# Joined two-block kernel: operand order of the passes at each stage's opening, an earlier start, and finer and moved steps beside the products

## The chip, the cores and the metric

One core of a Trainium2 chip. The metric is the device time of one launch in microseconds (us); lower is better. Engines: TensorE (PE), VectorE (DVE), ScalarE (ACT), GpSimd (POOL), and SyncE (SP), whose queue issues the DMAs.

## The reference

Batch 1, sequence 512, width 1024, all f32. Two blocks run one after the other, each of two layers; together they are six sublayers, the kernel's stages. Each takes a norm of x, computes, norms the result and adds it to x.

```python
def first_block(x, ...):                       # layers 0 and 1
        h = rms_norm(x, pre_norm_w[layer])
        y = even_mixer(h, ...)                 # layer 0: retention + stick-breaking attention
        y = odd_mixer(h, ...)                  # layer 1: hgrn2 + causal conv and rg_lru
        x = x + rms_norm(y, post_norm_w[layer])
def second_block(x, ...):                      # sandwich(h, pre, post, fn) = h + rmsnorm(fn(rmsnorm(h)))
    h = sandwich(h, ..., even_mixer_2)         # differential attention + conformer convolution
    h = sandwich(h, ..., swiglu)               # (silu(h @ w_gate) * (h @ w_up)) @ w_down, 1024 -> 2816 -> 1024
    h = sandwich(h, ..., odd_mixer_2)          # S5 state-space layer (256 channels) + latent attention, 6 heads
    h = sandwich(h, ..., swiglu)
```

The parts that the change touches: every projection `h @ w_in`; in `s5_ssm` the discretisation (`mag`, `cos`, `sin` of `li * dt`) and the linear recurrence over time of 1024 complex states; in `mla_attention` the softmax of each head, `softmax(q k^T)`, over key blocks of 64.

## The kernel before

The activations stay on chip, transposed: features on 128 partitions, 8 tiles `k` of 128 × 512. The weights come once, as a stream of 128 × 128 tiles in slots of 8 (512 KB): SP loads a slot into one of three buffers `raw`; ScalarE rounds it to fp32r, `wh` (`round_slot`, L624 to L630); GpSimd computes the remainder `wl = raw − wh` in four pieces (`split_slot`, L2627 to L2631). Activations are treated alike: `hh` is x times the norm's weight, rounded (ScalarE, L645), `hl` its remainder (VectorE, L693); inside a stage `mh`, `ml`. One product of a 128 × 128 weight tile with 512 tokens is three matmuls (passes) into one PSUM bank, in `product`, L569 to L578:

```python
            e.matmul(ps[b][:], a, xh, start=first, stop=False)
            e.matmul(ps[b][:], a, xl, start=False, stop=False)
            e.matmul(ps[b][:], l, xh, start=False, stop=final).then_inc(pe.sem, pe.up(*step))
```

The order of all work is a list of steps per stage (`STEPS`, from `steps_even`, `steps_odd`, `steps_diff`, `steps_ffn`, `steps_ssm`), written by hand. Every engine walks the same list and issues its share of each step into its own in-order queue; engines meet at semaphores alone. A step `("w", g, k)` is one product of group g (128 output features), `("e", g)` the eviction of g's bank, `claim` makes TensorE wait until the bank's last reader is done, and `BANKS` says which of eight banks a kind of group may use. `merge` (L96) interleaves lists evenly by their length, so that a list with more steps is spread at other places. The stages are `even`, `odd`, `diff`, `ffn0`, `ssm`, `ffn1`.

**Opening** (L133). Each stage begins with x's update by the stage before (`nx`, VectorE L679 and L682), then for each k: `hi` (ScalarE: `hh`, and the square of x, L645 and L648), `lo` (VectorE: `hl`), the products of three groups (two in ssm), and `sq`, a matmul of ones by the square (L605), which sums for the norm; `rs` turns the sum into a factor that the evictions apply. Block k means these steps of one k. TensorE waits for `lo` of k ahead of block k. The sums and evictions go to banks 0 to 3 and 7.

**Start of the kernel.** ScalarE (`scalar_program`, L2613) rounds the first three slots, then waits for `mats` (a table of 128 × 128 constants) and copies five of them to fp32r (`EXACT`, L2619), then enters `act_even`, which loads its function table (L981) and comes to `hi` 0. SP (`sync_program`, L2656) issues x in eight transfers, a slot after x1, x3 and x7, and `mats` after x3.

**ffn0.** Gate and up products (`fg`, `fu`) for a tile f, their evictions (`e1` to `e3`) beside the next tile's products, down products, and the closing (`o`, then `on`, the ones matmul of the post-norm). The eight steps `ds` compute the S5 layer's tables (VectorE, ScalarE, GpSimd) for the stage after; they are merged into the closing of ffn0.

**ssm.** Per pair of attention heads: projections `un`, `ur`, `kn`, `vw`; for two lanes at a time score products `r1` (L2123 to L2128), row maximum `r2` (VectorE L2335) and exponentials (ScalarE L2499), reciprocal `r3` (L2340, L2342), transposing products `r4` (L2137), values `v1`, `v2`. Beside it the scan over eight sets of 128 states: `s1` (TensorE L2158, L2159; VectorE L2356 to L2359, products with cosine and sine), `s2` (two sums L2365, L2367; two scans L2369, L2371), `s3` (four products and two sums, L2377 to L2386), `s4` (TensorE L2170, L2172), and after each four sets `z1` to `z4`, which end in the input of `zg`, the gate's product. Heads and scan are merged.

## Time and profile before

| | |
|---|---|
| median of 3 runs | 2041.15 us (2040.47 to 2041.37) |
| the profiled execution's own time | 2041.19 us |
| its span, first to last instruction | 2039.4 us |
| mean granted TensorE clock | 0.934 |
| busy: PE, PEld | 1795.7 us (88%) of 7412 matmuls, 1350.4 us (66%) |
| busy: DVE, ACT, POOL | 960.8 us (47%), 738.5 us (36%), 926.9 us (45%) |
| DMA | 139.89 MB, mean 69 GB/s |

The table is from one profiled execution. PE is the matmul itself and PEld its weight load, which overlaps with it. Busy shares are means over stages of different kinds; what bounds a place is read from the waits in it. The stages take roughly: even 0 to 340 us, odd to 660, diff to 950, ffn0 to 1335, ssm to 1645, ffn1 to the end. The granted clock is a share of full speed; its two levels are 1.2 and 2.4 GHz. In waits, "PE ps L576 <- DVE hl L693" is TensorE idle ahead of a matmul of line 576, released by the instruction of line 693 on VectorE.

### The profile page before, as it was taken

Reading aid. Unit: us, or ns where it says so; the run is one execution under the profiler, and the core shown is the slowest. Engines: PE = TensorE matmul, PEld = TensorE weight load, DVE = VectorE, ACT = ScalarE, POOL = GpSimd, SP = SyncE. Lnnn points to the kernel's source line nnn. Section 1 sums busy time; section 2 is a strip of 40 time slices with the busy share of each in tenths; the row PEclk is TensorE's granted clock in tenths of the full one; section 3 lists DMA queues with packets and bytes.
Section 4 is the critical chain, followed back from the end, with each engine's and each line's share of the span. In section 5 each row is a group of like instructions: output and inputs, shape, how many; then the busy total and the mean of one; then the engine's idle time right before and its main releaser. Section 6 shows DMA issues by size and latency. Waiting matters only on the chain.

```text
span 2039.4 us, 19949 instructions
## 1 busy us (share of the span) xinstructions
PE 1795.7 (88%) x7412; PEld 1350.4 (66%) x7412; DVE 960.8 (47%) x1483; ACT 738.5 (36%) x1207; POOL 926.9 (45%) x1100
## 2 busy tenths in 40 slices
PE   5999978988778888688999999978777889999996
PEld 3776556666665676456788888755444568888885
DVE  1043435675543699636321313655655554123244
ACT  4264554354344322454332222342222443322232
POOL 3433124465653444024565656467123336556563
PEclk9999999988988899898999999997778899999998
DMA  4311012122111122012232332211000112233231
GB/s 169 93 63 63 31 42 82 62 63 72 42 32 52 62 73 73 11 42 73 85 102 93 98 99 94 77 60 49 11 11 21 42 63 93 94 100 96 93 97 69
DMA packets 39553, 139.89 MB, mean 69 GB/s; under 512 B 4512, under 2 KB 4640, under 8 KB 39328
## 3 DMA queue, kind: packets, MB, share of 16 engines
q1 hardware_dynamic: 39456, 138.61, 21.3%
q8 instruction: 59, 0.97, 0.2%
q14 instruction: 38, 0.31, 0.1%
HBM read 136.50 MB, written 2.10 MB: 68 GB/s over the span
## 4 chain that ended last, share of the span: by engine, by line
PE 72%; DVE 17%; ACT 7%; issue 2%; POOL 1%; DMA 0%; SPq 0%; DVEq 0%; ACTq 0%; POOLq 0%
PE ps L576 18%; PE ps L577 18%; PE ps L578 18%; DVE ps L1734 3%; PE ps L605 2%; PE ps L589 1%; PE ps L2146 1%; PE ps L591 1%; PE ps L590 1%; PE ps L841 1%; PE ps L2123 1%; POOL wl L2631 1%; PE ps L1150 1%; PE ps L2137 1%; DVE arena L679 1%
## 5 line engine op out<-in xcount | busy, mean ns | idle before, releaser
L2631 POOL TENSOR_TENSOR wl<-raw,wh 128x256 fp32r<-128x256 f32 x988 | 802.8, 843 | 975.8 <-ACT wh L630 975.4
L576 PE MATMUL ps<-hh,wh 128*128 128x512 f32 x1204 | 518.3, 431 | 72.8 <-DVE hl L693 46.0
L577 PE MATMUL ps<-hl,wh 128*128 128x512 f32 x1204 | 479.1, 398 | 0.0
L578 PE MATMUL ps<-hh,wl 128*128 128x512 f32 x1204 | 478.7, 398 | 0.0
L630 ACT ACTIVATE wh<-raw 128x1024 fp32r<-128x1024 f32 x247 | 261.0, 1057 | 559.6 <-PE ps L578 511.2
L576 PEld LDWEIGHTS ps<-hh,wh 128*128 128x128 f32 x1204 | 232.9, 193 | 150.7 <-DVE hl L693 52.1
L576 PE MATMUL ps<-mh,wh 128*128 128x512 f32 x632 | 267.8, 424 | 48.5 <-DVE ml L937 7.8
L577 PEld LDWEIGHTS ps<-hl,wh 128*128 128x128 f32 x1204 | 232.7, 193 | 62.0 <-issue 17.7
L578 PEld LDWEIGHTS ps<-hh,wl 128*128 128x128 f32 x1204 | 232.0, 193 | 50.6
L577 PE MATMUL ps<-ml,wh 128*128 128x512 f32 x632 | 254.0, 402 | 0.0
L578 PE MATMUL ps<-mh,wl 128*128 128x512 f32 x632 | 253.8, 402 | 0.0
L576 PEld LDWEIGHTS ps<-mh,wh 128*128 128x128 f32 x632 | 123.2, 195 | 98.2 <-issue 12.1
L578 PEld LDWEIGHTS ps<-mh,wl 128*128 128x128 f32 x632 | 123.2, 195 | 27.1
L577 PEld LDWEIGHTS ps<-ml,wh 128*128 128x128 f32 x632 | 124.2, 196 | 23.8 <-issue 1.9
L1944 DVE TENSOR_TENSOR ml<-arena,mh 128x512 fp32r<-128x512 f32 x44 | 35.0, 795 | 119.4 <-ACT mh L1975 119.4
L1933 DVE TENSOR_TENSOR arena<-ps,nrm 128x512 f32<-128x512 f32 x44 | 30.4, 691 | 127.7 <-PE ps L578 127.7
L1734 DVE SCALAR_TENSOR_TENSOR ps<-arena,vec,ps 128x512 f32<-128x512 f32 x116 | 87.4, 753 | 2.9
L1931 DVE TENSOR_TENSOR arena<-ps,nrm 128x512 f32<-128x512 f32 x44 | 29.9, 680 | 100.0 <-PE ps L578 100.0
L693 DVE SCALAR_TENSOR_TENSOR hl<-x,vec,hh 128x512 fp32r<-128x512 f32 x48 | 40.2, 838 | 54.1 <-ACT hh L645 54.1
L589 PE MATMUL ps<-wh,hh 128*128 128x512 f32 x128 | 51.9, 405 | 9.3 <-DVE arena L1205 9.2
L661 ACT ACTIVATE nrm<-arena 128x512 f32<-128x512 f32 x48 | 30.1, 627 | 77.2 <-DVE arena L703 77.1
L605 PE MATMUL ps<-nrm,mats 128*128 128x512 f32 x96 | 53.4, 640 | 0.0
(464 smaller groups left out, 2223.6 us busy)
## 6 DMA issues: line engine op xcount, KB each, us to landing
raw<-in_w SPq DMA_DIRECT2D x247, 512.0 KB, 3.5
x<-in_x SPq DMA_DIRECT2D x8, 256.0 KB, 6.9
out<-x SPq DMA_DIRECT2D x8, 256.0 KB, 2.0
arena<-in_rope SPq DMA_DIRECT2D x3, 512.0 KB, 4.9
arena<-in_dec SPq DMA_DIRECT2D x1, 1024.0 KB, 11.3
mats<-in_mats SPq DMA_DIRECT2D x1, 576.0 KB, 7.9
arena<-in_lw SPq DMA_DIRECT2D x1, 512.0 KB, 3.8
arena<-in_levels SPq DMA_DIRECT2D x1, 448.0 KB, 4.5
```

The costliest lines, as they stand in the source:

```text
L576: e.matmul(ps[b][:], a, xh, start=first, stop=False)
L577: e.matmul(ps[b][:], a, xl, start=False, stop=False)
L578: e.matmul(ps[b][:], l, xh, start=False, stop=final).then_inc(pe.sem, pe.up(*step))
L589: e.matmul(ps[i][:], hh[:, k, cut(i)], a, start=(k == 0), stop=False)
L605: e.matmul(ps[7][:], M("ones"), sqr[k % 2], start=(k == 0), stop=(k == KT - 1)).then_inc(pe.sem, pe.up("sq", k))
L630: e.activation(wh[:, n % NHL, :], raw[:, n % NRAW, :], ACT.Copy).then_inc(rounded.sem, rounded.up(n))
L661: e.activation(sqr[d % 2], y[:, d, :], ACT.Square).then_inc(act.sem, act.up("oe", d))
L693: e.scalar_tensor_tensor(out=hl[:, k, :], in0=x[:, k, :], scalar=V(PRE[stage], k), in1=hh[:, k, :].bitcast(F32), op0=MUL, op1=SUB).then_in ...
L1734: e.scalar_tensor_tensor(out=yb[:, j, :] if q == 30 else conv_in[j], in0=du[:, j, q:q + T], scalar=V("dww", 4 * q + j), in1=conv_in[j], op ...
L1933: e.tensor_tensor(f_up[f % 2], ps[bank(stage, ("fu", f))][:], rb_pre, MUL).then_inc(dve.sem, dve.up("e", ("fu", f)))
L1944: e.tensor_tensor(ml[:, i, :], f_up[f % 2], mh[:, i, :].bitcast(F32), SUB).then_inc(dve.sem, dve.up("mixed", f))
L2631: e.tensor_tensor(wl[:, n % NHL, cut(i, 2)], raw[:, n % NRAW, cut(i, 2)], wh[:, n % NHL, cut(i, 2)].bitcast(F32), SUB).then_inc(split.sem, ...
```

## The change

1. **Openings.** In each block k of the opening of all six stages, the passes of the two or three groups are ordered by operand: first `wh`·`hh` of each group, then `wh`·`hl` of each, then `wl`·`hh` of each. The first kind waits for `hi` of k and, at a slot's start, for the rounding alone; the second for `lo` of k; the third, at a slot's start, for `wl`. Consecutive passes go to different banks.
2. **Start.** ScalarE loads the function table ahead of any wait; the three slots are rounded between the `hi` steps, the copies of `EXACT` stand ahead of `hi` 4. TensorE waits for these copies at the last ones matmul of the first stage instead of the first. SP issues a slot after x0, x1 and x3, and `mats` after x1's slot.
3. **ffn0.** The `ds` steps go into the gate and up groups of tiles 0 to 3, 5 and 7 to 9. The table preloaded at the end of step 4 is another one.
4. **ssm.** `s1` is cut in two steps, `s2` and `s3` in three each, and the list of the scan is ordered by hand around them. `merge` then places the pieces at other points between the heads' steps; the stage's list has 417 steps where it had 377.
5. **Banks.** In odd, the groups `gl`, `gg`, `hq` and `hf` may use banks 0 to 3 instead of 0 and 1.

The lists of even, odd, diff and ffn1 are as before.

```diff
@@ open_products, new; it is called at each stage's first "w" step of block k
+        def open_products(e, stage, k):
+            s, gs = S[stage], OPENS[stage]
+            e.wait_ge(s.act.sem, s.act["hi", k])
+            for g in gs:
+                step = ("w", g, k)
+                if k == 0:
+                    claim(e, bank(stage, g))
+                if (stage, step) in STARTS:
+                    e.wait_ge(rounded.sem, rounded[STARTS[stage, step]])
+                e.matmul(ps[bank(stage, g)][:], tile(stage, step)[0], hh[:, k, :], start=(k == 0), stop=False)
+            e.wait_ge(s.dve.sem, s.dve["lo", k])
+            for g in gs:
+                e.matmul(ps[bank(stage, g)][:], tile(stage, ("w", g, k))[0], hl[:, k, :], start=False, stop=False)
+            for g in gs:
+                step = ("w", g, k)
+                if (stage, step) in STARTS:
+                    e.wait_ge(split.sem, split["wl", STARTS[stage, step]])
+                e.matmul(ps[bank(stage, g)][:], tile(stage, step)[1], hh[:, k, :], start=False, stop=(k == KT - 1)).then_inc(
+                    s.pe.sem, s.pe.up(*step))
+                if k == KT - 1:
+                    busy[bank(stage, g)] = (s.dve, ("e", g))
@@ pe_norms, "sq"
                     if stage == "even":
                         e.wait_ge(s_mats, 16)
-                        e.wait_ge(consts.sem, consts[EXACT[-1]])
+                if stage == "even" and k == KT - 1:
+                    e.wait_ge(consts.sem, consts[EXACT[-1]])
@@ act_even (the preload and the loops leave scalar_program, whose first line is now the preload)
-            e.preload_act_table_set(EXP_LN)
...
+                if kind == "hi" and 1 <= step[1] <= NHL:
+                    round_slot(e, step[1] - 1)
+                if step == ("hi", NHL + 1):
+                    e.wait_ge(s_mats, 16)
+                    for name in EXACT:
+                        e.activation(R(name), M(name), ACT.Copy).then_inc(consts.sem, consts.up(name))
@@ sync_program
-                if k in (1, 3, 7):
-                    load_slot(e, k // 3)
-                if k == 3:
+                if k in (0, 1, 3):
+                    load_slot(e, (k + 1) // 2)
+                if k == 1:
                     e.dma_start(mats[:], io["mats"]).then_inc(s_mats, 16)
@@ STEPS
-"ffn0": steps_ffn(*[("ds", n) for n in range(8)]),
+"ffn0": steps_ffn(first=[("ds", 0)], f1=[("ds", 1)], f2=[("ds", 2)], f3=[("ds", 3)], f5=[("ds", 4)], f7=[("ds", 5)],
+                  f8=[("ds", 6)], f9=[("ds", 7)]),
@@ steps_ssm
-        scan += [("s1", i), ("s2", i), ("s1", i + 1), ("s3", i), ("s2", i + 1), ("s3", i + 1)]
+        scan += [("s1", i), ("s1b", i), ("s2", i), ("s2b", i), ("s1", i + 1), ("s1b", i + 1), ("s2c", i), ("s3", i), ("s3b", i)]
+        scan += [("s3c", i), ("s2", i + 1), ("s2b", i + 1), ("s2c", i + 1), ("s3", i + 1), ("s3b", i + 1), ("s3c", i + 1)]
@@ BANKS, "odd"
-"gl": (0, 1), "gg": (0, 1), "hq": (0, 1), "hf": (0, 1)
+"gl": (0, 1, 2, 3), "gg": (0, 1, 2, 3), "hq": (0, 1, 2, 3), "hf": (0, 1, 2, 3)
```

`s1b` holds the third and fourth product of `s1`, `s2b` and `s2c` the two scans, `s3b` the third and fourth product of `s3`, `s3c` its two sums.

**The queues.** TensorE at the kernel's start, block 0, before:

```order
L576 MATMUL ps0<-hh,wh 128x512 [waits weights_split,dve_even]
L577 MATMUL ps0<-hl,wh 128x512
L578 MATMUL ps0<-hh,wl 128x512
L576 MATMUL ps1<-hh,wh 128x512
L577 MATMUL ps1<-hl,wh 128x512
L578 MATMUL ps1<-hh,wl 128x512
L576 MATMUL ps2<-hh,wh 128x512
L577 MATMUL ps2<-hl,wh 128x512
L578 MATMUL ps2<-hh,wl 128x512
L605 MATMUL ps7<-nrm,mats 128x512 [waits act_even,constants_set,mats_landed]
```

and now:

```order
L599 MATMUL ps0<-hh,wh 128x512 [waits weights_rounded,act_even]
L599 MATMUL ps1<-hh,wh 128x512
L599 MATMUL ps2<-hh,wh 128x512
L602 MATMUL ps0<-hl,wh 128x512 [waits dve_even]
L602 MATMUL ps1<-hl,wh 128x512
L602 MATMUL ps2<-hl,wh 128x512
L607 MATMUL ps0<-hh,wl 128x512 [waits weights_split]
L607 MATMUL ps1<-hh,wl 128x512
L607 MATMUL ps2<-hh,wl 128x512
L638 MATMUL ps7<-nrm,mats 128x512 [waits act_even,mats_landed]
```

The same ten matmuls; those with `hl` and with `wl` now stand behind three that need neither, and the wait for all constants is off the first ones matmul.

ScalarE at the kernel's start, before:

```order
L630 ACT_TABLE_LOAD [waits weights_landed0]
L630 ACTIVATE wh<-raw 128x1024 [waits constants_set]
L630 ACTIVATE wh<-raw 128x1024 [waits weights_landed1]
L630 ACTIVATE wh<-raw 128x1024 [waits weights_landed2]
L2619 ACTIVATE mats_exact<-mats 128x128 [waits mats_landed]
L2619 ACTIVATE mats_exact<-mats 128x128 x4
L981 ACT_TABLE_LOAD [waits vec_landed]
L645 ACTIVATE hh<-x,vec 128x512 [waits x0_landed]
L648 ACTIVATE nrm<-x 128x512
L645 ACTIVATE hh<-x,vec 128x512 [waits x1_landed]
```

and now (L678 and L681 are `hi`, L663 the rounding):

```order
L2680 ACT_TABLE_LOAD
L678 ACTIVATE hh<-x,vec 128x512 [waits x0_landed,vec_landed,constants_set]
L681 ACTIVATE nrm<-x 128x512
L663 ACTIVATE wh<-raw 128x1024 [waits weights_landed0]
L678 ACTIVATE hh<-x,vec 128x512 [waits x1_landed]
L681 ACTIVATE nrm<-x 128x512
L663 ACTIVATE wh<-raw 128x1024 [waits weights_landed1]
L678 ACTIVATE hh<-x,vec 128x512 [waits x2_landed]
L681 ACTIVATE nrm<-x 128x512 [waits pe_even]
L663 ACTIVATE wh<-raw 128x1024 [waits weights_landed2]
L678 ACTIVATE hh<-x,vec 128x512 [waits x3_landed]
```

`hh` 0 stood behind two table loads, three roundings and five copies, and is now the second instruction; the roundings stand between the `hh`, and the copies of `mats` follow behind a fourth rounding, ahead of `hh` 4.

TensorE in ssm, where the second `s1` (L2158, L2159; now L2206, L2207) stands, before:

```order
L576 MATMUL ps0<-mh,wh 128x512 [waits act_ssm]
L577 MATMUL ps0<-ml,wh 128x512
L578 MATMUL ps0<-mh,wl 128x512
L2158 MATMUL ps6<-arena 128x512 [waits dve_ssm]
L2159 MATMUL ps7<-arena 128x512
L576 MATMUL ps0<-mh,wh 128x512
L577 MATMUL ps0<-ml,wh 128x512
L578 MATMUL ps0<-mh,wl 128x512
L2123 MATMUL ps2<-arena 128x384 [waits act_ssm,dve_ssm]
L2123 MATMUL ps3<-arena 128x384
```

and now:

```order
L587 MATMUL ps0<-mh,wl 128x512
L585 MATMUL ps1<-mh,wh 128x512 [waits dve_ssm]
L586 MATMUL ps1<-ml,wh 128x512
L587 MATMUL ps1<-mh,wl 128x512
L2206 MATMUL ps6<-arena 128x512 [waits dve_ssm]
L2207 MATMUL ps7<-arena 128x512
L2131 MATMUL ps0<-wh,mh 128x128 [waits weights_split,act_ssm]
L2132 MATMUL ps0<-wl,mh 128x128
L2133 MATMUL ps0<-wh,ml 128x128
```

It stood inside the products `un` of the second pair of heads, behind the first scores; it now stands behind the last `kn` of the first pair, ahead of `vw` (L2131 to L2133) and all scores.

VectorE in ssm, ahead of the row maxima (L2335; now L2383) of the third pair of score blocks; L2377 to L2386 is `s3` of the second set, now L2436 to L2452. Before:

```order
L2340 RECIPROCAL small<-small 128x1 [waits act_ssm]
L2342 TENSOR_SCALAR nrm<-mats,small 128x128 [waits dve_ssm]
L2377 TENSOR_TENSOR hh_scratch_49<-hh_scratch_49,mh_scratch_51 128x512 [waits dve_ssm]
L2379 TENSOR_TENSOR hl_scratch_50<-hl_scratch_50,mh_scratch_51 128x512 [waits dve_ssm]
L2381 TENSOR_TENSOR hl_scratch_50<-hl_scratch_50,ml_scratch_52 128x512 [waits dve_ssm]
L2382 TENSOR_TENSOR hh_scratch_49<-hh_scratch_49,ml_scratch_52 128x512
L2384 TENSOR_TENSOR hh_scratch_49<-hh_scratch_49,hl_scratch_50 128x512 [waits dve_ssm]
L2386 TENSOR_TENSOR hl_scratch_50<-hl_scratch_50,hh_scratch_49 128x512 [waits dve_ssm]
L2340 RECIPROCAL small<-small 128x1 [waits act_ssm]
L2342 TENSOR_SCALAR nrm<-mats,small 128x128 [waits dve_ssm]
L2335 TENSOR_REDUCE small<-ps2 128x1 [waits pe_ssm]
L2335 TENSOR_REDUCE small<-ps3 128x1 [waits pe_ssm]
```

and now:

```order
L2390 TENSOR_SCALAR nrm<-mats,small 128x128 [waits dve_ssm]
L2430 SCALAR_TENSOR_TENSOR hl_scratch_50<-small,hl_scratch_50 128x512 [waits dve_ssm]
L2388 RECIPROCAL small<-small 128x1 [waits act_ssm]
L2390 TENSOR_SCALAR nrm<-mats,small 128x128 [waits dve_ssm]
L2436 TENSOR_TENSOR hh_scratch_49<-hh_scratch_49,mh_scratch_51 128x512 [waits dve_ssm]
L2438 TENSOR_TENSOR hl_scratch_50<-hl_scratch_50,mh_scratch_51 128x512 [waits dve_ssm]
L2444 TENSOR_TENSOR hl_scratch_50<-hl_scratch_50,ml_scratch_52 128x512 [waits dve_ssm]
L2445 TENSOR_TENSOR hh_scratch_49<-hh_scratch_49,ml_scratch_52 128x512
L2383 TENSOR_REDUCE small<-ps2 128x1 [waits pe_ssm]
L2450 TENSOR_TENSOR hh_scratch_49<-hh_scratch_49,hl_scratch_50 128x512 [waits dve_ssm]
L2452 TENSOR_TENSOR hl_scratch_50<-hl_scratch_50,hh_scratch_49 128x512 [waits dve_ssm]
L2383 TENSOR_REDUCE small<-ps3 128x1 [waits pe_ssm]
```

The first row maximum moves ahead of the two sums of `s3`, the second stays behind all six instructions.

## Rows read from the trace of the kernel before

**Rows 1.** The page's part 4, whole span: share by engine.
```profile
PE 72%; DVE 17%; ACT 7%; issue 2%; POOL 1%; DMA 0%; SPq 0%; DVEq 0%; ACTq 0%; POOLq 0%
```

**Rows 2.** Waits of TensorE, whole span: us in total, times, longest.
```profile
PE ps L576 <- DVE hl L693: 46.0, 6, 21.0
PE ps L2123 <- ACT nrm L2499: 27.6, 6, 6.4
```

**Rows 3.** Timeline, kernel's start: start us, us, engine line, output <- inputs [idle before <- releaser].
```profile
7.72 1.28 ACT L630 ACT_TABLE_LOAD   x1 [7.72 <-DMA raw<-in_w]
...
10.15 5.49 POOL L2631 TENSOR_TENSOR wl<-raw,wh 128x256 fp32r<-128x256 f32 x8 [9.71 <-ACT wh L630]
...
19.39 0.72 ACT L645 ACTIVATE hh<-x,vec 128x512 fp32r<-128x512 f32 x1
...
21.03 0.79 PE L576 MATMUL ps<-hh,wh 128*128 128x512 f32 x1 [21.03 <-DVE hl L693]
...
25.95 0.96 PE L576 MATMUL ps<-hh,wh 128*128 128x512 f32 x1
```

**Rows 4.** The tile mats, 0 to 60: from issue to landing, us.
```profile
DMA to landing us min/median/max: 7.9/7.9/7.9
```

**Rows 5.** DMA view, 0 to 60, in 40 slices of 1.5 us.
```profile
GB/s 0 221 184 300 325 405 418 398 410 411 431 415 404 344 289 85 0 0 0 0 0 0 0 0 60 289 0 0 11 38 292 19 0 0 0 82 265 3 0 33
```

**Rows 6.** Timeline, opening of the stage odd.
```profile
339.70 0.72 ACT L645 ACTIVATE hh<-x,vec 128x512 fp32r<-128x512 f32 x1 [1.54 <-DVE x L682]
...
341.77 0.79 PE L576 MATMUL ps<-hh,wh 128*128 128x512 f32 x1 [5.00 <-DVE hl L693]
...
355.75 0.80 PE L576 MATMUL ps<-hh,wh 128*128 128x512 f32 x1
...
358.70 0.80 PE L576 MATMUL ps<-hh,wh 128*128 128x512 f32 x1
```

**Rows 7.** Windows: stretch, sum, PE, PEld, DVE, ACT, POOL busy, PEclk, DMA share, GB/s.
```profile
337.00:347.00 10.00, 5.23 (x12) 3.81 (x12) 8.67 (x11) 5.17 (x8) 3.65 (x4) 0.67 0.29 98
```

**Rows 8.** The same view, body of ffn0.
```profile
1100.00:1150.00 50.00, 50.00 (x222) 41.41 (x221) 16.95 (x22) 13.78 (x18) 30.84 (x36) 1.00 0.30 95
```

**Rows 9.** Waits of TensorE, 1290 to 1345, closing of ffn0.
```profile
PE ps L576 <- DVE arena L703: 2.8, 3, 1.6
PE ps L576 <- POOL wl L2631: 1.7, 2, 1.0
PE ps L616 <- DVE nrm L711: 1.3, 1, 1.3
```

**Rows 10.** Windows view and timeline, ssm, the merged heads and scan.
```profile
1395.00:1612.00 217.00, 171.26 (x587) 103.99 (x586) 132.60 (x216) 54.83 (x122) 64.48 (x60) 0.77 0.06 18
...
1419.30 0.69 DVE L2356 TENSOR_TENSOR hh_scratch<-ps,mh_scratch 128x512 f32<-128x512 f32 x1 [6.37 <-PE ps L2159]
...
1440.64 0.75 DVE L2335 TENSOR_REDUCE small<-ps 128x1 f32<-128x256 f32 x2
...
1443.04 0.55 PE L2123 MATMUL ps<-arena 128*128 128x128 f32 x1 [5.02 <-ACT nrm L2499]
...
1487.49 0.98 PE L2123 MATMUL ps<-arena 128*128 128x384 f32 x1 [5.35 <-ACT nrm L2499]
...
1544.24 0.56 PE L2123 MATMUL ps<-arena 128*128 128x384 f32 x1 [3.48 <-ACT nrm L2499]
...
1570.42 0.55 PE L2123 MATMUL ps<-arena 128*128 128x128 f32 x1 [6.37 <-ACT nrm L2499]
```

**Rows 11.** Timeline of VectorE, ssm, first and last of the last z chain.
```profile
1598.48 0.75 DVE L2392 SCALAR_TENSOR_TENSOR arena<-arena,vec,ps 128x512 f32<-128x512 f32 x1 [3.06 <-PE ps L2172]
...
1611.90 1.15 DVE L2414 TENSOR_TENSOR hl<-arena,hh 128x512 fp32r<-128x512 f32 x1 [0.70 <-ACT hh L2532]
```

**Rows 12.** Timeline of TensorE, stage odd, two waits for an eviction.
```profile
477.40 0.80 PE L589 MATMUL ps<-wh,hh 128*128 128x512 f32 x1 [9.02 <-DVE arena L1205]
...
532.68 0.80 PE L576 MATMUL ps<-hh,wh 128*128 128x512 f32 x1 [5.61 <-DVE arena L1205]
```

82 lines of the change are left out of this document (55 added, 27 removed), and 2 rows, old and new, of the table BANKS.

## Prediction

> **What bounds the kernel now.** I read the chain of waits first. TensorE holds 72% of the chain that ended last, VectorE 17%, ScalarE 7% [rows 1]: this is a matmul-bound kernel with holes, and only two things save time, fewer holes in TensorE's work or a clock that is granted in full for longer. Next, TensorE's waits, to see which holes there are. The largest is `product` waiting for `hl`, the remainder of the activations, 46.0 us in six times of which one is 21.0 [rows 2]. So the start of the kernel costs 21.0 and each of the five later stage openings 5.0. Second is the wait for the softmax exponentials in the ssm stage, 27.6 us in six. Third I read one window per place that the change touches.
>
> **Start of the kernel.** ScalarE sits until the first weights are there (7.72), loads a table, rounds three slots, waits for `mats`, copies it, loads a second table, and comes to the first `hh` at 19.39; TensorE starts at 21.03 and leaves block 0 at 25.95 [rows 3]. Only the first slot is needed for that block.
>
> Now: the table load comes before any wait, `hh` 0 needs only x0, then slot 0 is rounded. x0, half as large, stands right ahead of slot 0 in SP's queue, so `hh` 0 and its square are done before the weights come. One x less (256 KB) stands ahead of slot 0 than before, and the transfers run at 300 to 430 GB/s without a break from 4.5 to 21 us [rows 5], so its landing moves from 7.7 to about 7.2. Rounding 1.06 gives 8.3: the three passes of rounded weights with `hh` start there, the three with `hl` follow (6 × 0.43 slow-clock passes = 2.6, to 10.9), and the weights' remainder is there at 8.3 + 4 × 0.69 (5.49/8 in [rows 3]) = 11.05. Three passes more end at 12.35. The ones matmul needs `mats`: it is issued behind x1 and slot 1, two x earlier than before, near 3.1, and 7.9 from issue to landing [rows 4] give 11.0, no wait. It takes 1.05 (21.03 to 25.95 is 4.92, less nine passes of 0.43), so block 1 starts at 13.4 instead of 25.95: 12.55 earlier.
>
> A part is given back at block 4. `hh` 4 now stands behind the rounding of slot 3 and the five copies of `mats`. Slot 3's raw data is about 6 MB down the queue, at 410 GB/s some 16 us, and with its start and the pauses of the queue 19 to 20; + 1.06 (a rounding) + 1.1 (five small copies, taken as one rounding) + 0.72 = 21.9 to 22.9 for `hh` 4, and TensorE gets there at 13.4 + 3 × 2.95 = 22.25. I take 0.55 of stall. **−12.0**, bounds −10.5 (slot 0 lands at 8.8, the stall 1.1) and −13.
>
> **Openings.** [Rows 6] show the second stage's; the four others look the same. ScalarE has `hh` 0 at 340.42; TensorE starts at 341.77, released by `hl` 0, after 5.00 of idling. Its passes are 0.43 apart at first (341.77 to 346.69 for block 0, as long as at the kernel's start), which is 1.2 GHz, and 0.23 later, 2.4 GHz; the granted clock is 0.67 over 337 to 347 [rows 7]. Full-speed blocks are 355.75 to 358.70, 2.95 apart, and never wait: from block 1 on `hh` and `hl` are ahead. So all that the new pass order releases is the first block's head. Three passes need only `hh`: they start at 340.48 instead of 341.77, run 3 × 0.43 = 1.29, and `hl` is there as they end. Four openings × 1.29 and ssm's, with two groups, 0.86: **−6.0**. The clock falls as before, since TensorE still idles 3.7, and recovers as much earlier as work starts earlier. Bounds: if it recovered at the old moment, the early passes would save only half, −3. If it did not fall at all, each opening would save another 2.3 (9 × 0.20 plus half of the ones matmul's 1.05), together −17.5.
>
> Later blocks write banks 0, 1, 2 in turn instead of three passes each. What does a change of bank cost? The ffn body changes bank at each product's end, and 222 matmuls fill its 50.00 us [rows 8]: 0.225 each, where 512 columns at 2.4 GHz are 0.213. If all of the 0.012 excess were bank changes, one in three matmuls, a change would be 0.036, and the 272 added ones 9.8 us. But a block of the openings, with a change at one pass in three, is no slower per pass than the body: 2.95 [rows 6] less a ones matmul of two half-rate passes (0.9) is 0.228 for each of nine. I take 0, with 9.8 as bound. The Trainium skill, "TensorE: Matmul & The Clock Gate", section "A second HAM failure mode: psum-queue depth-cycling", speaks against this order: a kernel that cycles through PSUM banks each iteration had TensorE idling briefly so often that its clock went up and down. The body's row, cycling at every third pass with the clock at 1.00, does not show it; at every pass no run here shows it. By that rule it is the slower rival below.
>
> **ffn0.** The eight `ds` steps stood in the closing, where TensorE waited 2.8 for `arena`, 1.7 for `wl` and 1.3 for `nrm` [rows 9], waits that ffn1's closing, the same without `ds`, does not have. They move under gate and up groups, where TensorE is busy 50.00 of 50.00 while VectorE is at 34% and ScalarE at 28% [rows 8]. **−5.8**, bounds −4 and −6. If that cover failed, the `e` steps would free banks later and nothing would be gained. The other table preloaded replaces one load by one: 0.
>
> **ssm.** The window 1395 to 1612 holds the merged heads and scan: TensorE idles 46 of 217 us at clock 0.77 [rows 10]. The waits come from VectorE's in-order queue: the row maxima (reduces) at 1440.64 stand behind two scans and six products of the scan, the exponentials wait for them and TensorE for those, 5.02 at 1443.04. Before that VectorE had idled 6.37 waiting for TensorE's two s1 matmuls (1419.30): they now stand ahead of the first `vw` and the first scores, so that work is done while VectorE had none, and in pieces of one or two instructions the first reduce of a pair stands two products earlier. Walking the gaps 1443.04, 1487.49, 1544.24, 1570.42 [rows 10] (20.2 together) in the new order: −3.4, −4, −2.5, −3.5, together −13.4. Against it: s1 ahead of the first `vw` delays the first scores by their two matmuls at slow clock, +1.5, and the last z chain starts later: today it runs 1598.48 to 1611.90 [rows 11] beside the output products, and its end releases `zg`; about 2 of it would come out from cover. **−10**, bounds −25 (the clock recovers too over part of the window) and +5.
>
> **odd banks.** Gates and hq/hf get four banks for two. TensorE waited 9.02 and 5.61 for `arena` [rows 12], evictions that freed a bank; but what sets the pace there is VectorE's own chain, so most of that returns at the next need. I take **−3**, bounds 0 and −12.
>
> **Sum.** 12.0 + 6.0 + 5.8 + 10 + 3 = 36.8 off the profiled execution's 2041.19 (0.04 above the median of the runs): **2004.4**, say 2004.
>
> **Rivals.**
> 1. The ssm reorder and the banks bring next to nothing, because VectorE's busy sum there (132.6 of 217 [rows 10]) is unchanged and each released wait is met at the next in-order step (the second reduce of the pair at 1440.64 still stands behind all six products). Start, openings and ffn0 remain: 23.8, 2017; with part of it, 2013 to 2022. For it: these are the terms got by walking, not by a row. 0.22.
> 2. ssm backfires: z's chain exposed in full, 13.4 [rows 11], or a scan standing before each reduce. 2041.2 − 23.8 + 5 to 13: 2022 to 2032. 0.08.
> 3. The pass order releases nothing, since another wait (bank, rounded weights) ends as late: 6 less and part of the start, 2010 to 2017. 0.04.
> 4. The clock: with idling cut from 5.0 to 3.7 the openings may keep it, −11.5, and ssm at 0.77 has room, its 171 busy us shrinking by up to 10 at a fuller clock. 1980 to 1995. 0.18.
> 5. Slower: changing banks at every pass makes TensorE pause, and the clock goes with it. The openings' 408 passes would run at 0.43 instead of 0.225: 83.7 us dearer, 2088. It decides from 36.8/408 = 0.09 us per pass on. Against it are the body's rows. 0.03.
> Mine, 1995 to 2013, gets 0.45. A measurement of this kernel can tell about 0.2% (4 us) from no change, so 2037 to 2045 is "same": 0.01, only by a partial rival 5. Faster 0.95, slower 0.04. The range, 1983 to 2025, takes in rivals 1 and 3, most of 4 and a third of 2.
>
> **What would show it.** TensorE's wait for `hl` should all but vanish and be replaced by one for `hh`, 3.7 per opening; the first matmul at 8.3 and block 1 at 13.4; blocks still 2.95 apart (more than 3.3 is rival 5); ffn0's three closing waits gone; TensorE's busy time unchanged within 5 us and ssm's window at about 205 instead of 217. I am wrong if ssm's waits for the exponentials stay at 27 (rival 1), if the wait for `zg` after the last z chain exceeds 8 (rival 2), or if the first matmul comes later than 10.

## The result, and the profile after

The changed kernel takes 2005.74 us (median of 4, 2000.34 to 2006.59) against 2041.26 (median of 4): ratio 0.9819, interval 0.9801 to 0.9838, 35.5 us faster. The forecast was 2004, in 1983 to 2025. The profiled execution took 2006.59 us, its span is 34.6 us shorter than before's.

The page of the changed kernel, its head and the chain that ended last:

```profile
span 2004.8 us, 19949 instructions
...
PE 1793.1 (89%) x7412; PEld 1346.4 (67%) x7412; DVE 969.6 (48%) x1483; ACT 738.6 (37%) x1206; POOL 931.4 (46%) x1100
...
PE 72%; DVE 16%; ACT 6%; POOL 2%; issue 2%; DMA 1%; SPq 0%; DVEq 0%; ACTq 0%; POOLq 0%
```

TensorE's share of the chain is the same as in [rows 1], of a shorter span. Its waits over the whole span (us in total, times, longest):

```profile
PE ps L599 <- ACT hh L678: 20.1, 6, 3.7
...
PE ps L2171 <- ACT nrm L2565: 12.9, 6, 4.2
...
PE ps L2171 <- ACT arena L2565: 10.6, 3, 7.1
...
PE ps L621 <- DVE arena L1247: 8.8, 1, 8.8
...
PE ps L585 <- POOL wl L2693: 8.7, 3, 5.3
...
PE ps L599 <- ACT wh L663: 7.8, 1, 7.8
```

The wait for `hl` of [rows 2] is gone; 20.1 for `hh` and 7.8 for the first rounded slot stand in its place. The exponentials of ssm held TensorE for 27.6 and now hold it for 12.9 in one form and 10.6 in the other, which was 1.5 before. Of the 8.7 for the weights' remainder, all in odd, before has nothing; its own 1.7 [rows 9] were in ffn0 and are gone.

Where the 34.6 us came from. I took two milestones of each stage in both traces: the last sum of its opening (the small matmul of the step `rs`, L610, now L643) and the ones matmul of its post-norm (L616, now L649), and how much earlier each comes:

| milestone | before | now | earlier by | gained since the line above | forecast |
|---|---|---|---|---|---|
| even, opening's end | 48.60 | 37.86 | 10.74 | 10.74 | 12.0 |
| even, post-norm | 333.98 | 326.64 | 7.34 | −3.40 | 0 |
| odd, opening's end | 369.54 | 360.02 | 9.52 | 2.18 | 1.29 |
| odd, post-norm | 658.06 | 648.13 | 9.93 | 0.41 | 3 |
| diff, opening's end | 693.59 | 681.22 | 12.37 | 2.44 | 1.29 |
| diff, post-norm | 944.91 | 931.41 | 13.50 | 1.13 | 0 |
| ffn0, opening's end | 980.50 | 964.52 | 15.98 | 2.48 | 1.29 |
| ffn0, post-norm | 1331.28 | 1307.75 | 23.53 | 7.55 | 5.8 |
| ssm, opening's end | 1360.71 | 1336.80 | 23.91 | 0.38 | 0.86 |
| ssm, post-norm | 1641.25 | 1607.88 | 33.37 | 9.46 | 10 |
| ffn1, opening's end | 1676.83 | 1642.32 | 34.51 | 1.14 | 1.29 |
| ffn1, post-norm | 2021.46 | 1986.91 | 34.55 | 0.04 | 0 |

The start, in the timeline of the changed kernel (start us, us, engine line, [idle before <- releaser]):

```profile
6.57 1.06 ACT L663 ACTIVATE wh<-raw 128x1024 fp32r<-128x1024 f32 x1 [0.54 <-DMA raw<-in_w]
...
7.77 1.62 PE L599 MATMUL ps<-hh,wh 128*128 128x512 f32 x3 [7.77 <-ACT wh L663]
...
11.01 1.65 PE L607 MATMUL ps<-hh,wl 128*128 128x512 f32 x3 [0.34 <-POOL wl L2693]
...
13.01 1.26 PE L599 MATMUL ps<-hh,wh 128*128 128x512 f32 x3
...
21.22 1.06 ACT L663 ACTIVATE wh<-raw 128x1024 fp32r<-128x1024 f32 x1 [4.07 <-DMA raw<-in_w]
...
22.18 1.09 ACT L1024 ACTIVATE mats_exact<-mats 128x128 fp32r<-128x128 f32 x5
...
23.94 0.98 PE L599 MATMUL ps<-hh,wh 128*128 128x512 f32 x3 [1.59 <-ACT hh L678]
```

TensorE starts at 7.77 where [rows 3] have 21.03, waits 0.34 for the weights' remainder, and is at block 1 at 13.01 instead of 25.95. Of these 12.9 us, 1.59 are given back at block 4, behind the fourth rounding (21.22) and the constants (22.18).

The opening of odd, in the timeline:

```profile
333.14 1.35 PE L599 MATMUL ps<-hh,wh 128*128 128x512 f32 x3 [3.70 <-ACT hh L678]
...
337.51 1.27 PE L599 MATMUL ps<-hh,wh 128*128 128x512 f32 x3
```
and in the windows view (stretch, its length, busy us of PE, PEld, DVE, ACT and POOL, PEclk, DMA share, GB/s):

```profile
328.37:338.37 10.00, 6.30 (x15) 3.68 (x16) 7.38 (x10) 5.63 (x9) 2.35 (x3) 0.83 0.32 112
```

TensorE idles 3.70 instead of 5.00 [rows 6], and block 0 lasts 4.37 us (333.14 to 337.51) instead of 4.92: the clock is back sooner. The ten microseconds that begin 4.77 before TensorE's start have a granted clock of 0.83; [rows 7] are the same ten around before's opening, 0.67. From one stage's post-norm to the next opening's end, the windows view of before has granted clocks of 0.90 (odd, diff, ffn0, ffn1) and 0.88 (ssm); now they are 0.95 in odd, diff and ffn0, and 0.90 in ffn1 and 0.88 in ssm as before.

ffn0's closing and the start of ssm's opening, TensorE's waits from 1265 to 1320; the three of [rows 9] are gone, and one of 0.6 behind the post-norm's first ones matmul is new:

```profile
PE ps L599 <- ACT hh L678: 3.7, 1, 3.7
PE ps L651 <- ACT nrm L694: 0.6, 1, 0.6
```

In ssm, the stretch from the opening's end to the post-norm, first before, then now (windows view):

```profile
1360.71:1641.25 280.54, 227.27 (x815) 147.10 (x816) 159.83 (x249) 82.06 (x157) 108.24 (x108) 0.82 0.09 29
```

```profile
1336.80:1607.88 271.08, 223.59 (x814) 145.00 (x815) 164.51 (x249) 82.31 (x157) 112.12 (x108) 0.83 0.10 30
```

280.54 us with 53.3 of idle TensorE became 271.08 with 47.5. One of the waits that grew, in the timeline of the changed kernel:

```profile
1401.14 1.55 DVE L2450 TENSOR_TENSOR hh_scratch<-hh_scratch,hl_scratch 128x512 f32<-128x512 f32 x1
...
1402.61 1.74 DVE L2452 TENSOR_TENSOR hl_scratch<-hl_scratch,hh_scratch 128x512 f32<-128x512 f32 x1
...
1405.27 0.55 DVE L2383 TENSOR_REDUCE small<-ps 128x1 f32<-128x384 f32 x1
...
1405.73 1.08 DVE L2416 TENSOR_TENSOR hh_scratch<-hh_scratch 128x512 f32<-128x512 f32 x1
...
1406.74 1.75 DVE L2418 TENSOR_TENSOR hl_scratch<-hl_scratch 128x512 f32<-128x512 f32 x1
...
1408.40 0.55 DVE L2383 TENSOR_REDUCE small<-ps 128x1 f32<-128x384 f32 x1
...
1409.04 0.58 ACT L2565 ACTIVATE arena<-ps,small 128x384 f32<-128x384 f32 x1 [2.53 <-DVE small L2383]
...
1409.82 2.04 PE L2171 MATMUL ps<-arena 128*128 128x256 f32 x4 [7.11 <-ACT arena L2565]
```

L2383 is the row maximum, L2416 and L2418 are sums of the scan, L2450 and L2452 the last of the set before. The second maximum of the pair (1408.40) stands behind the two sums (1405.73 and 1406.74), the first (1405.27) behind the two before; the exponentials follow and TensorE has idled 7.11, where the same matmul waited 1.11 before (at 1431.74). It is the kind of wait that [rows 10] show at 1443.04, at another pair.

### The profile page after: what moved, and what is told of

Its sections match the earlier page's. It is cut to its first block, busy times and chain, and to the rows that moved or that the text cites. A ratio compares the mean times of both kernels' runs of the same rounds, so it can differ in the third digit from the quotient of the medians.

```text
span 2004.8 us, 19949 instructions
## 1 busy us (share of the span) xinstructions
PE 1793.1 (89%) x7412; PEld 1346.4 (67%) x7412; DVE 969.6 (48%) x1483; ACT 738.6 (37%) x1206; POOL 931.4 (46%) x1100
## 4 chain that ended last, share of the span: by engine, by line
PE 72%; DVE 16%; ACT 6%; POOL 2%; issue 2%; DMA 1%; SPq 0%; DVEq 0%; ACTq 0%; POOLq 0%
PE ps L585 17%; PE ps L587 17%; PE ps L586 17%; DVE ps L1778 4%; PE ps L638 2%; PE ps L602 2%; PE ps L599 2%; PE ps L607 2%; POOL wl L2693 1%; PE ps L621 1%; PE ps L622 1%; PE ps L623 1%; PE ps L876 1%; PE ps L2171 1%; PE ps L2194 1%
## 5 line engine op out<-in xcount | busy, mean ns | idle before, releaser
L663 ACT ACTIVATE wh<-raw 128x1024 fp32r<-128x1024 f32 x247 | 260.9, 1057 | 573.4 <-PE ps L587 512.6
L585 PE MATMUL ps<-hh,wh 128*128 128x512 f32 x1068 | 441.3, 413 | 21.7 <-POOL wl L2693 8.7
L586 PE MATMUL ps<-hl,wh 128*128 128x512 f32 x1068 | 421.5, 395 | 0.0
L587 PE MATMUL ps<-hh,wl 128*128 128x512 f32 x1068 | 421.3, 394 | 0.0
L586 PEld LDWEIGHTS ps<-hl,wh 128*128 128x128 f32 x1068 | 204.5, 191 | 46.4 <-issue 6.8
L587 PEld LDWEIGHTS ps<-hh,wl 128*128 128x128 f32 x1068 | 203.7, 191 | 44.0
L587 PEld LDWEIGHTS ps<-mh,wl 128*128 128x128 f32 x632 | 123.5, 195 | 27.3
L599 PE MATMUL ps<-hh,wh 128*128 128x512 f32 x136 | 61.3, 559 | 27.9 <-ACT hh L678 20.1
L599 PEld LDWEIGHTS ps<-hh,wh 128*128 128x128 f32 x136 | 27.4, 207 | 55.5 <-issue 27.3
```

What stands on the lines that cost most here:

```text
L599: e.matmul(ps[bank(stage, g)][:], tile(stage, step)[0], hh[:, k, :], start=(k == 0), stop=False)
L663: e.activation(wh[:, n % NHL, :], raw[:, n % NRAW, :], ACT.Copy).then_inc(rounded.sem, rounded.up(n))
```

## The experiments

Twelve kernels. Medians of one kernel differ by up to 3.5 us between sets of runs (before: 2041.8, 2044.7, 2041.3, 2043.2 in the four sets, and 2037 to 2047 in single runs), so where a part is worth a few us I read the stretches of its trace.

**The start alone.** The edits of point 2 of the change, on the kernel before, with the old `product` in the openings.

```diff
+            e.preload_act_table_set(EXP_LN)
             e.wait_ge(consts.sem, consts["set", 2])
-            for n in range(NHL):
-                round_slot(e, n)
...
-                if k in (1, 3, 7):
-                    load_slot(e, k // 3)
+                if k in (0, 1, 3):
+                    load_slot(e, (k + 1) // 2)
```

> The start's part alone (table load first, roundings between the hi steps, slots and constants issued earlier), with the old pass order. Theory: TensorE must still wait for the weights' remainder of slot 0, so it starts near 11 instead of 7.8, block 1 near 15.9 instead of 25.95, and nothing stalls at block 4, because hh 4 (ready near 24) comes before TensorE does: 10.0 us faster than before. Rival (the start gains only with the new pass order, since the remainder is what is late): under 5 us. Second rival: the stall at block 4 is there as well and limits the gain to the 10.7 of the whole change, so both are within 1 us of one another.

2030.24 us against 2041.8, ratio 0.9938 (0.9915 to 0.9961). Its timeline:

```profile
11.27 0.77 PE L582 MATMUL ps<-hh,wh 128*128 128x512 f32 x1 [11.27 <-POOL wl L2639]
...
15.36 0.80 PE L582 MATMUL ps<-hh,wh 128*128 128x512 f32 x1
...
25.26 0.50 PE L582 MATMUL ps<-hh,wh 128*128 128x512 f32 x1 [0.56 <-DVE hl L700]
```

TensorE waits for the weights' remainder till 11.27 and is at block 1 at 15.36; block 4 (25.26) waits 0.56 for `hl`. At the opening's end it is 9.91 us ahead of before, the changed kernel 10.74. The theory has the size (10.0) but said that nothing stalls at block 4; the second rival, a stall there as well and the two kernels within 1 us, holds. The new pass order starts TensorE 3.5 us sooner and brings block 1 forward by 2.35, and at block 4 the changed kernel stalls 1.59 where this one stalls 0.56. The other 7 us by which this profiled execution was ahead came in ssm, which it does not touch; see below.

**The pass order alone.** `open_products` in all six openings, on the kernel before.

```diff
-                    if g == ("lx", 0):
-                        e.wait_ge(dve.sem, dve["lo", k])
+                    if g in OPENS["odd"]:
+                        if g == OPENS["odd"][0]:
+                            open_products(e, "odd", k)
+                        continue
```

> The new pass order in all six openings alone. Forecast's term: 6.0 us faster, 1.29 in each of four openings and 0.86 in ssm, plus about 0.9 at the kernel's start, 6.9 in all. Theory after the trace of the whole change, where the openings of odd, diff and ffn0 gave 2.2 to 2.5 each: block 0 also ends its slow stretch sooner, so 8.5 to 9.5. Rival (a change of bank costs 0.036 us a pass): 9.8 less, no gain or slower.

2034.17 us against 2041.8, ratio 0.9955 (0.994 to 0.9971): 7.6 us faster by the medians, 9.2 by the ratio. By milestones the openings gave 0.91, 2.45, 2.07, 2.43, 0.92 and 2.43, together 11.2; 1.9 were lost in the body of odd. So an opening is worth more than the 1.29 us of its three early passes, and the granted clock tells where: in odd, diff, ffn0 and ffn1, from post-norm to opening's end, it is 0.95 here for before's 0.90. ffn1's opening shows both cases in the eight kernels with this order: 1.98 to 2.43 us gained in the four whose clock there is 0.95, and 1.14 to 1.41, about the early passes alone, in the four with 0.90.

**Banks in turn, old waits.** The same order of passes, but nothing may start earlier. The lines are against the kernel of the pass order alone; the later waits for `lo` and for `wl` go.

```diff
-            e.wait_ge(s.act.sem, s.act["hi", k])
+            e.wait_ge(s.dve.sem, s.dve["lo", k])
...
-                    e.wait_ge(rounded.sem, rounded[STARTS[stage, step]])
+                    e.wait_ge(split.sem, split["wl", STARTS[stage, step]])
```

> The same order of passes, but each block waits for what it waited for before (hl and the weights' remainder ahead of its first pass), so that only the turning of banks is left of this part. Theory: a change of bank is free, within 1 us of before, blocks of the openings 2.95 us apart at full clock as before. Rival (TensorE pauses at each change of bank): up to 9.8 us slower than before, a block 3.2 us; with the clock going down as well, over 80 us slower.

2042.66 us (10 runs) against 2041.8 (13 runs), ratio 1.0002 (0.9992 to 1.0012). Its timeline in the opening of odd:

```profile
354.71 1.26 PE L596 MATMUL ps<-hh,wh 128*128 128x512 f32 x3
...
357.65 1.26 PE L596 MATMUL ps<-hh,wh 128*128 128x512 f32 x3
```

A block at full clock takes 2.94 us (354.71 to 357.65), the 2.95 of [rows 6]. A change of bank at every pass costs nothing that can be measured, and the granted clock of the openings is before's (0.90, ssm 0.88); the slower rival falls. The case of the Trainium skill that the prediction weighed ("TensorE: Matmul & The Clock Gate", "A second HAM failure mode: psum-queue depth-cycling") is another one: there TensorE idled briefly between groups of matmuls, while here the banks change inside an unbroken run of passes.

The surprise is elsewhere: at the even stage's post-norm this kernel is 4.55 us behind before, though it was 0.72 ahead at the opening's end and nothing differs in between. The same stretch in three kernels (before, this one, the changed kernel), which run the same list of instructions there:

```profile
48.60:333.98 285.38, 265.74 (x1117) 187.20 (x1117) 98.12 (x195) 130.89 (x240) 98.31 (x132) 0.97 0.19 59
```

```profile
47.88:338.53 290.65, 270.99 (x1117) 189.99 (x1117) 98.23 (x195) 130.95 (x240) 98.26 (x132) 0.95 0.18 58
```

```profile
37.86:326.64 288.78, 269.36 (x1116) 189.06 (x1117) 98.12 (x195) 130.98 (x240) 98.23 (x132) 0.96 0.19 59
```

TensorE idles 19.6, 19.7 and 19.4 us in them, and the same waits last equally long in each; but it is busy 265.7, 271.0 and 269.4 us for the same matmuls, with a granted clock of 0.97, 0.95 and 0.96. After each wait of some microseconds a slow stretch follows or does not, and how long it is changes from execution to execution. This is the 3.40 that the change seems to lose in even. The kernel of the next experiment shows it more plainly: up to ffn0 it is before itself, and its even stretch is 290.59 us with 19.7 idle, 5.2 longer. In its trace 27.3 us of that stretch stand at 1.2 GHz, in before's 17.1; half of the difference is 5.1. Over all fourteen traces the stretch takes 283.4 to 290.6 us (mean 287.6), so before's is a short one.

**ds alone.** Point 3 of the change.

```diff
-"ffn0": steps_ffn(*[("ds", n) for n in range(8)]),
+"ffn0": steps_ffn(first=[("ds", 0)], f1=[("ds", 1)], f2=[("ds", 2)], f3=[("ds", 3)], f5=[("ds", 4)], f7=[("ds", 5)],
+                  f8=[("ds", 6)], f9=[("ds", 7)]),
```

> The ds steps alone moved from ffn0's closing into its gate and up groups. Forecast's term: 5.8 us faster. The trace of the whole change shows 7.55 for the stretch from ffn0's opening to its post-norm; if all of that is this part, 7.5. Rival (the evictions beside the gate and up products get late and the gain is half lost): 3 us or less.

2032.53 us against 2041.8, ratio 0.995 (0.9935 to 0.9965). The stretch from ffn0's opening to its post-norm is 7.55 us shorter, to the hundredth what the changed kernel shows; 0.63 is given back right behind, where the second ones matmul of the post-norm now waits. The body takes the steps without a gap:

```profile
1100.00:1150.00 50.00, 50.00 (x223) 41.40 (x222) 21.57 (x34) 14.71 (x18) 30.76 (x36) 1.00 0.32 96
```

VectorE's share is 43% where [rows 8] have 34%, TensorE is busy 50.00 of 50.00. The 7.55 are more than the 5.87 us that TensorE idles there before. The rest is in the matmuls next to each wait, as the trace of before shows at the first one:

```profile
1304.47 0.39 PE L578 MATMUL ps<-mh,wl 128*128 128x512 f32 x1
1305.91 0.50 PE L576 MATMUL ps<-mh,wh 128*128 128x512 f32 x1 [1.04 <-DVE arena L703]
1306.25 0.40 PE L577 MATMUL ps<-ml,wh 128*128 128x512 f32 x1
```

Starts are 0.23 apart in an unbroken run. Here they are 1.44 and 0.34 apart, 1.78 for two steps that take 0.46 without a wait: 1.32 us for an idle time of 1.04. The five waits inside the products cost 0.27 us each beyond their idle time, 1.4 together; the sixth is ahead of the post-norm.

**The scan alone.** Point 4 of the change.

```diff
-        scan += [("s1", i), ("s2", i), ("s1", i + 1), ("s3", i), ("s2", i + 1), ("s3", i + 1)]
+        scan += [("s1", i), ("s1b", i), ("s2", i), ("s2b", i), ("s1", i + 1), ("s1b", i + 1), ("s2c", i), ("s3", i), ("s3b", i)]
+        scan += [("s3c", i), ("s2", i + 1), ("s2b", i + 1), ("s2c", i + 1), ("s3", i + 1), ("s3b", i + 1), ("s3c", i + 1)]
```

> The scan's steps cut and reordered, alone. Forecast's term: 10 us faster. Theory after reading five traces whose ssm list is the old one (TensorE idles 52.8 to 54.3 us between the openings' last sum and the post-norm of that stage, in 273.5 to 280.5 us, a spread of 7 that no edit explains) and the whole change's (47.5 us idle in 271.0): the reorder removes 6 us of idling and the stretch takes 269 to 273 us, so about 6 us faster by medians, with 7.11 still idle at a wait for the exponentials of the second pair. Rival (all 9.5 us seen in the trace are the reorder's): the stretch at 267 or less. Rival (the clock gave them all): idling stays above 52.

2034.22 us against 2044.73, ratio 0.995 (0.9932 to 0.9968). The stretch of ssm:

```profile
1363.35:1634.41 271.06, 223.97 (x815) 145.25 (x815) 164.35 (x249) 82.30 (x157) 111.86 (x108) 0.83 0.10 31
```

271.06 us with 47.1 idle, the changed kernel's 271.08 and 47.5. The six kernels that keep the old list take 273.6 to 280.5 us there (mean 277.5) with 52.8 to 54.3 idle. The three kernels with the new list as it stands take 271.06 to 271.32. So by the traces the reorder is worth 6.4 us of that stretch, as the theory had it, and the remaining 3 of the 9.46 are before's own execution, one of the two longest. The medians say more, 10.5 us, with an interval of 6.5 to 13.9 by the ratio: the traces' figure lies at its lower end.

**The banks alone.** Point 5.

```diff
-"gl": (0, 1), "gg": (0, 1), "hq": (0, 1), "hf": (0, 1)
+"gl": (0, 1, 2, 3), "gg": (0, 1, 2, 3), "hq": (0, 1, 2, 3), "hf": (0, 1, 2, 3)
```

> Four banks for gl, gg, hq and hf in the odd stage, alone. Forecast's term: 3 us faster, bounds 0 and 12. Theory after the trace of the whole change: TensorE runs ahead at once, and there waits 8.7 us in three times for the weights' remainder (GpSimd), which it had not waited for before; the waits for evictions only change places, so within 0.5 us of before at the odd stage's post-norm.

2041.67 us (10 runs) against 2044.73 (13 runs), ratio 0.999 (0.998 to 0.9999). TensorE's waits from 365 to 600:

```profile
PE ps L1156 <- DVE arena L1350: 10.0, 11, 3.0
...
PE ps L595 <- DVE arena L1211: 8.8, 1, 8.8
...
PE ps L582 <- POOL wl L2637: 8.4, 3, 5.3
```

The two of [rows 12] are among six waits for L1205's evictions before, 22.5 us; one of 8.8 is left. In their stead TensorE waits 8.4 us for GpSimd's remainder, before 0, and 10.0 for another eviction (L1350), before 3.7. The odd stage, from its opening's end to its post-norm, takes 288.79 us, before 288.52. The part alone gives nothing in its own stretch; the 3 us between the medians, with an interval that just excludes 0, have no place in it.

**Late rounding and constants**, an attempt to take back the stall at block 4 of the changed kernel.

```diff
-                round_ahead(e, "even", step)
+                if STARTS.get(("even", step)) != 1:
+                    round_ahead(e, "even", step)
...
-                if step == ("hi", NHL + 1):
+                if step == ("hi", 6):
+                    round_slot(e, NHL)
+                if step == ("hi", 7):
```

> The changed kernel with the fourth rounding put behind hi 6's place and the five copies of constants ahead of hi 7, so that hi 4 and hi 5 no longer stand behind them. Theory: the 1.59 us of TensorE at block 4 go, and with them all that the start gave back: block 8's end 1.6 us earlier than in the changed kernel, nothing later gets late, since slot 3 is used first behind the opening. Rival (another thing holds block 4, the square or the x transfer): less than 0.5 us.

2003.89 us, ratio 0.9801 (0.9782 to 0.982); the opening's end 12.03 us ahead of before, the changed kernel's 10.74:

```profile
14.00 1.30 PE L599 MATMUL ps<-hh,wh 128*128 128x512 f32 x3
...
22.85 1.26 PE L599 MATMUL ps<-hh,wh 128*128 128x512 f32 x3
```

Block 4 starts 8.85 us after block 1, without a wait, where the changed kernel took 10.93 (13.01 to 23.94). The first slot landed later in this execution (block 1 at 14.00), so that of the 2.1 us 1.29 are seen at the opening's end. Executions differ here as well: the opening's end is 10.45 to 11.81 us ahead of before in the three kernels with the early rounding, and 11.85 to 13.11 in the four with the late one.

**The scan behind the row maxima**, on the changed kernel: every piece of the scan and of z that stands between a score product `r1` and the second row maximum `r2` of its pair moves behind that maximum.

```diff
+def behind_rows(steps):
+    out = list(steps)
+    for n in range(0, 24, 2):
+        a, b = out.index(("r1", n)), out.index(("r2", n + 1))
+        part = out[a:b + 1]
+        late = [v for v in part if v[0] in ("s1", "s1b", "s2", "s2b", "s2c", "s3", "s3b", "s3c", "s4", "z1", "z2", "z3", "z4")]
+        out[a:b + 1] = [v for v in part if v not in late] + late
+    return out
...
-    out += merge(mul, scan)
+    out += behind_rows(merge(mul, scan))
```

> The changed kernel with the scan's pieces that stand between a score product and the second row maximum of its pair put behind that maximum, in all twelve pairs. Theory: what TensorE waits for in ssm are the maxima behind scan work on VectorE, so its two kinds of waits ahead of the scores (12.9 and 10.6 us in the changed kernel) fall to under 15 together, and the stage is 5 to 8 us shorter. Rival (VectorE's sum of work sets the pace, 149 of 232 us, and the wait moves to the scan's own chain): the scores' waits fall, but others grow by as much, 0 to 2 us.

1988.8 us, ratio 0.9728 (0.9705 to 0.9751), 17 us off the changed kernel. Its waits from 1331 to 1587:

```profile
PE ps L2195 <- ACT arena L2583: 7.5, 9, 3.2
...
PE ps L2181 <- ACT nrm L2575: 7.1, 3, 5.5
...
PE ps L2195 <- DVE nrm L2400: 4.0, 2, 2.9
...
PE ps L2181 <- ACT arena L2575: 2.1, 3, 1.2
```
and its stretch of ssm:

```profile
1331.04:1586.95 255.91, 215.79 (x814) 140.46 (x815) 164.26 (x249) 81.44 (x157) 109.77 (x108) 0.86 0.10 33
```

The two waits ahead of the scores are 7.1 and 2.1 where they were 12.9 and 10.6, others grew (7.5 for the eviction ahead of the transposing products, 4.0 for the reciprocals), idling is 40.1 for 47.5, and the stretch is 15.2 us shorter, twice what the idling says: TensorE's busy time fell by 7.8 us as well, at a clock of 0.86 for 0.83. This is more than the 5 to 8 us expected.

**Both**, the late rounding and the scan behind the row maxima.

> The two improvements together: the late fourth rounding and constants, and the scan's pieces behind the row maxima. Theory: they act 1300 us apart and add up, 1.6 + 15.2 us off the changed kernel by their own stretches, 1988 to 1990 where the changed kernel has 2005.7. Rival (the clock's dips move and take part back): anything up to 5 us off that, with the stretch of the scan still at 254 to 258 us and TensorE's idle time there at 40.

1991.84 us, ratio 0.9754 (0.9733 to 0.9775). The stretch of ssm is 255.77 us with 38.9 idle, the opening's end 12.24 us ahead; both parts are there. The even stage took 288.11 us where the kernel above had 283.39, and diff's 3.5 more, both untouched. The median lies 2 us above the theory's 1988 to 1990, inside what the rival on the clock allowed.

**The scan uncut, behind the row maxima.** The same rule, on the changed kernel with point 4 undone (the steps s1, s2, s3 whole and in their old order).

> The changed kernel with the scan's steps uncut, in the order before, but with every piece of the scan between a score product and the second maximum of its pair put behind that maximum. Theory: what counts is what a maximum stands behind, not how fine the scan's steps are: the stage's stretch is within 4 us of the 255.9 of the cut list with the same rule, idling 40 to 44. Rival (the cut matters by itself, since whole steps hold up the reciprocals and the values between two maxima): over 264.

1980.66 us, ratio 0.9709 (0.9688 to 0.973). Its stretch of ssm:

```profile
1333.21:1579.29 246.08, 201.71 (x815) 134.33 (x816) 165.49 (x249) 81.04 (x157) 110.07 (x108) 0.90 0.11 34
```
and in the timeline its longest wait there, for the scan's last sum:

```profile
1532.74 1.92 PE L2227 MATMUL ps<-hh_scratch,arena 128*32 128x512 f32 x4 [11.30 <-DVE hl_scratch L2443]
```

Both expectations missed on the good side: 246.08 us. The cut is not needed; with the rule it costs 8.7 us (255.8 and 255.9 in the two kernels that have it, 246.1 and twice 247.7 in the three without). TensorE idles more (44.4 for 40.1), but in fewer and longer pieces, one of 8.03 us and one of 11.3, and its clock is 0.90 for 0.86: 201.7 busy us for the same matmuls where the cut list had 215.8. Which of the two does it, the pieces of TensorE's waits or the phase in which they fall, these runs do not tell apart.

**The uncut scan with the late rounding.**

> The uncut scan behind the row maxima (as e10), and the late fourth rounding and constants (as e7). Theory: the scan's stretch again 246 us and the start 1.3 to 1.6 us earlier than in the changed kernel; if both hold, 1979 us, give or take the 4 us by which medians of one kernel differ between calls. Rival (the scan's 246 us with clock 0.90 was one lucky phase of the clock): the stretch at 250 to 256 us and 1983 to 1989 us.

1981.84 us, ratio 0.9695 (0.9681 to 0.971). The stretch of ssm is 247.71 us with 44.2 idle at clock 0.89, so it was no lucky execution; the opening's end is 13.11 us ahead, 2.4 more than the changed kernel and the largest of the study, where 1.3 to 1.6 were expected. This is the lowest ratio of the study, 61 us under before and 24 under the changed kernel. Against the kernel without the late rounding it is even within the intervals.

**The same with the old banks of odd.**

> As e11, with the odd stage's banks as they were before the change. Theory: the banks are worth nothing: the stretch of the odd stage from the last sum of its opening to its post-norm is 288.5 to 289 us against 287.8 to 288.1, and the whole within 1 us of e11. Forecast's term (3 us for the banks): 3 us slower than e11.

1983.52 us, ratio 0.9705 (0.9688 to 0.9723), 1.7 us above the last one, inside both intervals. The odd stage here:

```profile
358.43:649.08 290.65, 241.62 (x1068) 192.80 (x1069) 171.30 (x258) 127.33 (x227) 156.39 (x172) 0.88 0.16 51
```
and in the last kernel, with four banks:

```profile
359.72:647.85 288.13, 238.83 (x1069) 188.28 (x1069) 170.82 (x258) 127.23 (x227) 156.41 (x172) 0.91 0.16 52
```

With two banks it is 2.5 us longer, where the theory had 0.4 to 1.2. With the old pass order four banks were worth nothing (288.79 for 288.52); with the new one, two banks take 290.4 and 290.65 us in the two kernels that have them, four 287.8 to 288.1 in six. TensorE idles as long, 49.0 to 50.0, so again it is the clock (0.88 for 0.91) after waits that fall otherwise. So the four banks are worth the 1.9 us that the pass order alone had lost in odd, and the changed kernel shows 0.41 for both together.

## Why the prediction was right

The total, 36.8 forecast and 35.5 measured, is closer than the terms deserve, and partly by luck: three terms were too large, two too small, one loss was not forecast, and two stretches of before's own trace nearly cancel (even 2 us shorter than the mean of all traces, ssm 3 us longer than the mean of its list).

- **Start, −12.0.** Right in mechanism and steps: first matmul at 7.77 (8.3 forecast), remainder at 11.01 (11.05), block 1 at 13.01 (13.4). The ones matmuls took 0.56 ahead of block 1, where 1.05 was taken. The stall at block 4 was forecast at 0.55 and is 1.59, since slot 3 was rounded only from 21.22; the term is 10.74.
- **Openings, −6.0.** The mechanism is right (TensorE waits for `hh`, 3.70 to 3.71), the term mis-sized: 8.6 by the five milestones. The step that failed is "The clock falls as before, since TensorE still idles 3.7, and recovers as much earlier as work starts earlier". In odd, diff and ffn0 the clock lost about half as much as before (granted 0.95 for 0.90, and block 0 of odd lasts 4.37 instead of 4.92 us), and these gave 2.2 to 2.5 each. ffn1's kept 0.90 and gave 1.14, near the 1.29 forecast. ssm's gave 0.38; by itself the pass order gives 0.92 there, and the moved `ds` steps take 0.63 back.
- **A change of bank, 0.** Right, shown by itself.
- **ffn0, −5.8.** 7.55 in two kernels, outside the bounds of 4 and 6. TensorE's waits that I had summed are right: it idles 5.87 us from 1270 to the post-norm before, and not at all now. The other 1.7 are in the passes, 238 in 55.41 busy us before and 256 in 57.75 now (0.233 and 0.226 each), at a clock of 1.00 in both: what each wait costs beyond its idle time, 0.27 us, the term had put at nothing. Right behind, 0.63 is given back, so the part nets 6.9.
- **ssm, −10.** 9.46 in the trace, but 6.4 against the mean of six old-list executions, and 10.5 by the medians of the part alone. The walk was right where it looked: its four gaps fell from 20.2 to 7.8, by 12.4 of the 13.4 forecast (1443.04 from 5.02 to 1.43, 1487.49 from 5.35 to 1.96, 1544.24 from 3.48 to 1.27, 1570.42 from 6.37 to 3.15). It left the other waits ahead of score products at their old size. One of them fell (1424.02, 3.93 to 0.82), and four rose by 9.8 together, above all 1431.74, from 1.11 to 7.11, and 1551.80, from 0.43 to 2.96. What remained had stood in rival 1, that the second maximum of a pair still stands behind all six instructions of the scan (four products and two sums): moving the scan behind the maxima gave another 15 us. The z chain cost 3.3 us, where about 2 had been added: TensorE waits 2.69 and 0.61 at `zg`'s products, before not at all. That is far from the 8 of rival 2. To `zg`'s first product the stage is 10.8 us shorter, 206 for the window of 217, where 205 was forecast.
- **odd banks, −3.** 0.41 in the trace and nothing by itself; worth 2.5 only together with the pass order. The wait moved to the weights' remainder, which the term had not named.
- **Not forecast:** 3.40 lost in even, where TensorE idles as long and no instruction moved behind the opening; that is the clock's. And 1.13 gained in diff, where TensorE idles 38.8 us for 40.2. It is not the pass order's: two kernels with the old order idle 38.9 there, and two with the new one idle 40.3 and take 253.7 us. What makes the difference was not traced.

Rival 4 (the clock) is true as a mechanism, in small portions of both signs: in three openings the shorter wait kept part of the clock. Rival 1 holds for the banks alone; 2, 3 and 5 fall.

## What to carry to other kernels

Where one in-order engine serves both a critical chain and a filler, let the filler yield at each link of the chain (here: nothing of the scan between a score product and its row maxima) before cutting it finer; in the stage's stretch the cut gave 6 us against the mean of the old list, the rule without the cut 30. Moving work under a stage in which TensorE is never idle was free here and returned more than the waits that it removed (6.9 us for 5.87). Measure a part by the stretch of the trace that it acts on, against several executions of the untouched stretch: a single one here differs by up to 7 us from another.
